# Hybrid decoder block on one core: the first modulation by quarters of its weight, half of each sum on the tensor engine, and x loaded first

## The chip, the cores and the metric

One program on one core of a Trainium2 chip. The metric is the device time of one execution in microseconds (us). PE is the tensor engine (PEld its weight loads), DVE the vector engine, ACT the scalar engine, POOL the GpSimd engine, SP the engine that issues almost all DMAs from one queue in program order.

## The reference

One decoder block on x of 1024 tokens by 1024 features, all float32. The change touches only its first lines:

```python
mod = (jax.nn.silu(c) @ w_ada[l] + b_ada[l]).astype(x.dtype)[:, None, :]
sh1, sc1, gt1, sh2, sc2, gt2 = jnp.split(mod, N_MOD, axis=-1)

h = rms_norm(x, g_pre_mix[l]) * (1.0 + sc1) + sh1
proj = h @ w_in[l]
```

c is one row of 1024 numbers, w_ada is 1024 x 6144. The columns 0 to 2047 of `mod` are sh1 (shift) and sc1 (scale): the first modulation, 8 MB of weight. `proj` then feeds sparse attention, a pooling mixer, a merge, the output projection and a squared-ReLU MLP of width 4096; those parts take all but about the first 80 us of 1478 and are not edited.

## The kernel before

The kernel is written for each engine as one program, with semaphores by name. Features lie in eight blocks of 128 (KT = 8, index k), tokens in two halves of 512 (CH).

What happens ahead of the projections, in order:

- SP loads c, sixteen pieces of w_ada (`ada_piece`: one k block by 1024 columns, 512 KB; scale part first), then four tiles of x (the first half of the tokens), the weight `wv_raw` of values and gates, the other four tiles of x, and two blocks of `w_in` into `raw`.
- DVE multiplies each piece by its 128 values of silu(c) and adds it to `ada_acc` [128 x 2048] (L1423). The sum over the 128 partitions is then made by PE in `mod_columns`: `ada_acc` as weights, a column of ones as the moving side (L2075), once for scale and once for shift, and DVE turns the result into `scale` and `shift`.
- ACT squares x with a running sum (`square_x`, L973), POOL makes the inverse root (`x_rstd_of`, L813 and L815), DVE multiplies x by it (`normalise_x`, L1415).
- PE transposes each block of four 128 x 128 squares (`x_transposes(n)`, n = 0 to 7 for the first half, 8 to 15 for the second, L2085). ACT applies scale and shift on the way out of PSUM (`h_tmp`, L998), DVE splits the result into `act_hi` and `act_lo` (`split_h`, L1439 and L1441), so that a float32 product can be made from three fp32r products.
- `values_and_gates(ch, k)`: 12 products of 280 columns (four token tiles by three, L2062 to L2064), for half 0 and all k, then half 1. `v_evict` and `v_split` empty the result.
- `project` makes the feature-major blocks a = 0, 1, ... for rotary, compression, pooling and gates. They need all of `act_hi` and `act_lo`, that is, everything above.

After the last transpose POOL clears `acc2` and SP starts the weight of the second modulation (L500), which DVE adds in between the projections.

The lines that set the order on PE are few:

```python
mod_columns(0)
for n in range(8):
    x_transposes(n)
pe.wait_ge(mod_done, 2)
for k in range(KT):
    pe.wait_ge(wv_lo_s, k // 2 + 1)
    values_and_gates(0, k)
```

A matmul call on two float32 operands that is no transpose (L2075, L2169) shows as two instructions in the trace; calls on fp32r operands and transposes show as one.

Of the kernel before, what the change touches and what calls it, by code (L numbers as in the profile page):

```python
# [21 lines left out]
P = 128  # L22
KT = D_MODEL // P
# [119 lines left out]
def hybrid_block(nc, A, out):  # L143
# [64 lines left out]
    ada = place("ada", 154, [P, 8, 1024], f32)  # L208
# [117 lines left out]
    ada_added, mod_mm, mod_done = sem("ada_added"), sem("mod_mm"), sem("mod_done")  # L326
# [113 lines left out]
    def _(sp):  # L440
# [14 lines left out]
        def ada_piece(n):  # L455
            if n >= 8:
                sp.wait_ge(ada_added, n - 7)
            k, part = n % KT, 1 - n // KT
            sp.dma_start(ada[:, n % 8, :], w_ada[k * P:(k + 1) * P, part * 1024:(part + 1) * 1024]) \
              .then_inc(wide_in[n % 8], 16)  # L460
# [20 lines left out]
        sp.wait_ge(ada_added, 16)  # L481
# [304 lines left out]
    def _(pool):  # L786
# [35 lines left out]
        for i in range(4):  # L822
# [3 lines left out]
            if i:  # L826
                x_rstd_of(3 + i)
        x_rstd_of(7)
# [123 lines left out]
    def _(act):  # L952
# [36 lines left out]

        act.wait_ge(wv_in, 32)  # L990
        wv_split(0)
        act.wait_ge(mod_done, 2)
        for n in range(2 * KT):
            act.wait_ge(xt_mm, n + 1)
            if n >= 2:
                act.wait_ge(h_lo, n - 1)
            k = n % KT
            act.activation(h_tmp[:, n % 2, :], ps[:, n % 4, :], ACT.Identity, scale=scale[:, k:k + 1],  # L998
                           bias=shift[:, k:k + 1]).then_inc(h_made, 1)
            if n < 3:  # L1000
                wv_split(n + 1)
            if 1 <= n < 5:
                square_x(n + 3)
# [395 lines left out]
    def _(dve):  # L1399
# [11 lines left out]
        dve.wait_ge(silu_steps, 3)  # L1411
        dve.wait_ge(acc_bias, 16)
# [4 lines left out]
        for n in range(16):  # L1417
            dve.wait_ge(wide_in[n % 8], 16 * (n // 8 + 1))
            if n % KT:
                dve.wait_ge(ada_added, n)  # L1420
            k, part = n % KT, 1 - n // KT
            sl = slice(part * 1024, (part + 1) * 1024)
            dve.scalar_tensor_tensor(out=ada_acc[:, sl], in0=ada[:, n % 8, :], scalar=silu_c[:, k:k + 1],  # L1423
                                     in1=ada_acc[:, sl], op0=ALU.mult, op1=ALU.add).then_inc(ada_added, 1)
            if n == 10:
                dve.wait_ge(mod_mm, 1)
                dve.wait_ge(g_pre_in, 16)
                dve.scalar_tensor_tensor(out=scale, in0=ps[:, 7, 8:16], scalar=1.0, in1=g_pre, op0=ALU.add,
                                         op1=ALU.mult).then_inc(mod_done, 1)
        for t in range(3):  # L1430
            normalise_x(t)
        dve.wait_ge(mod_mm, 2)
        dve.tensor_copy(shift, ps[:, 7, 0:8]).then_inc(mod_done, 1)
        normalise_x(3)
# [13 lines left out]
        for n in range(2 * KT):  # L1448
            split_h(h_tmp, n, h_made, h_hi, h_lo)
            if 4 <= n < 8:  # L1450
                normalise_x(n)
# [1032 lines left out]
```

## Time and profile before

| What | us |
|---|---|
| Median of 3 runs | 1479.71 (1479.65 to 1481.0) |
| The profiled execution, its own time | 1479.39 |
| Span of its trace | 1477.6 |
| PE busy in the trace | 1411.5 (96%) |
| DVE busy | 1072.4 (73%) |
| PE busy in the first 20 us | 0 |
| PE busy from 20 to 40 us | 10.79 |

The span is the profiled execution from its first to its last instruction, 1.8 us less than that execution's own time. Most of the span is PE working without a gap; the change lies in the first 80 us. The trace gives a granted clock of PE by stretch: 1.00 is 2.4 GHz, 0.50 is 1.2 GHz. It records no change of it before 44.5 us.

### The profile page before, as it was taken

How to read it: one execution, taken by the hardware profiler on the slowest of the kernel's cores; microseconds unless marked ns; L12 is line 12 of the kernel's file. 1: busy time of each engine (PE TensorE's matmuls, PEld its weight loads, DVE VectorE, ACT ScalarE, POOL GpSimd, SP SyncE). 2: the span in 40 equal slices, each digit the busy share in tenths (PEclk: the TensorE clock that was granted, in tenths of full speed). 3: DMA queues.
4: the chain of work that ended last, by engine and by line, in shares of the span. 5: the costliest groups of instructions: out<-in, count | busy, mean ns of one | idle time of the engine just before them, and what ended most of it. 6: DMA issues, size and time to landing. Idle time of an engine off the chain costs nothing.

```text
span 1477.6 us, 19523 instructions
## 1 busy us (share of the span) xinstructions
PE 1411.5 (96%) x7206; PEld 1181.3 (80%) x7206; DVE 1072.4 (73%) x1483; ACT 637.2 (43%) x1112; POOL 332.3 (22%) x429
## 2 busy tenths in 40 slices
PE   2897999999999999989999999999999999999997
PEld 2886878888888888768887877888888888888885
DVE  6668844677877878885432788877777797777778
ACT  1534434555665656663123664222222434343342
POOL 3324432333322322111210410000000030404034
PEclk9998999999999999999999999999999999999999
DMA  9377956322221211016453424544443773535226
GB/s 350 82 243 260 274 120 168 89 70 65 61 65 44 59 54 35 19 63 193 144 185 100 143 73 158 198 157 156 147 144 137 270 287 112 199 110 204 87 84 228
DMA packets 131750, 208.31 MB, mean 141 GB/s; under 512 B 19525, under 2 KB 84549, under 8 KB 128071
## 3 DMA queue, kind: packets, MB, share of 16 engines
q1 hardware_dynamic: 128074, 196.61, 40.3%
q0 software_dynamic: 3584, 10.49, 2.1%
q8 instruction: 56, 0.92, 0.3%
q14 instruction: 36, 0.29, 0.1%
HBM read 146.24 MB, written 54.53 MB: 136 GB/s over the span
## 4 chain that ended last, share of the span: by engine, by line
PE 84%; DVE 8%; issue 3%; ACT 2%; DMA 1%; SPq 1%; POOL 1%; DVEq 0%; POOLq 0%; ACTq 0%
PE ps L2062 19%; PE ps L2064 18%; PE ps L2063 18%; PE ps L2068 5%; PE ps L2070 5%; PE ps L2069 5%; PE ps L2257 4%; PE ps L2273 2%; PE ps L2274 2%; PE ps L2224 2%; PE ps L2225 2%; DVE pt_lo L1606 1%; DVE acc L1550 1%; DVE ada_acc L1423 1%; DVE negm L1615 1%
## 5 line engine op out<-in xcount | busy, mean ns | idle before, releaser
L2062 PE MATMUL ps<-act_hi,a_hi 128*128 128x512 f32 x448 | 190.9, 426 | 0.9 <-DVE a_lo L1402 0.9
L2064 PE MATMUL ps<-act_hi,a_lo 128*128 128x512 f32 x448 | 175.8, 392 | 0.0
L2063 PE MATMUL ps<-act_lo,a_hi 128*128 128x512 f32 x448 | 175.2, 391 | 0.0
L2062 PE MATMUL ps<-wr_hi,left_hi 128*128 128x512 f32 x320 | 124.5, 389 | 0.0
L2063 PE MATMUL ps<-wr_lo,left_hi 128*128 128x512 f32 x320 | 124.5, 389 | 0.0
L2064 PE MATMUL ps<-wr_hi,left_lo 128*128 128x512 f32 x320 | 124.5, 389 | 0.0
L1606 DVE TENSOR_TENSOR pt_lo<-ps,pt_hi 128x512 fp32r<-128x512 f32 (+1 forms) x160 | 102.9, 644 | 20.0 <-ACT pt_hi L1141 18.7
L1323 ACT ACTIVATE left_hi<-left_st 128x2048 fp32r<-128x2048 f32 x28 | 53.6, 1915 | 144.4 <-PE ps L2064 81.5
L1243 ACT ACTIVATE w_hi<-w1s 128x1024 fp32r<-128x1024 f32 x54 | 57.0, 1057 | 112.1 <-PE ps L2064 74.8
L1141 ACT ACTIVATE pt_hi<-ps 128x512 fp32r<-128x512 f32 (+1 forms) x160 | 89.0, 563 | 32.8 <-PE ps L2257 31.1
L1730 DVE TENSOR_TENSOR w_lo<-w1s,w_hi 128x1024 fp32r<-128x1024 f32 x54 | 65.9, 1221 | 51.1 <-ACT w_hi L1243 51.0
L1615 DVE TENSOR_REDUCE negm<-ps 128x1 f32<-128x640 f32 (+7 forms) x128 | 89.3, 698 | 18.1 <-PE ps L2230 17.9
L876 POOL TENSOR_SCALAR ssum<-ssum 128x1 f32<-128x1 f32 (+1 forms) x160 | 41.7, 261 | 265.8 <-ACT p_win L1122 137.0
L2064 PEld LDWEIGHTS ps<-act_hi,a_lo 128*128 128x128 f32 x448 | 84.2, 188 | 18.4
L929 POOL TENSOR_TENSOR y<-y,u 128x512 f32<-128x512 f32 x36 | 59.0, 1666 | 168.7 <-DVE u L1971 151.4
L2062 PEld LDWEIGHTS ps<-act_hi,a_hi 128*128 128x128 f32 x448 | 85.2, 190 | 12.8 <-issue 2.1
L2063 PEld LDWEIGHTS ps<-act_lo,a_hi 128*128 128x128 f32 x448 | 85.1, 190 | 9.4
L1899 DVE TENSOR_TENSOR left_lo<-left_st,left_hi 128x2048 fp32r<-128x2048 f32 x28 | 64.1, 2291 | 37.8 <-ACT left_hi L1323 37.8
L927 POOL COPY y<-u 128x512 f32<-128x512 f32 x12 | 13.1, 1123 | 345.5 <-DVE u L1971 342.7
L2062 PE MATMUL ps<-am_hi,w_hi 128*128 128x512 f32 x192 | 75.5, 393 | 1.0 <-ACT h2f L1208 1.0
L2064 PE MATMUL ps<-am_hi,w_lo 128*128 128x512 f32 x192 | 74.7, 389 | 0.0
L2063 PE MATMUL ps<-am_lo,w_hi 128*128 128x512 f32 x192 | 74.7, 389 | 0.0
(279 smaller groups left out, 3874.5 us busy)
## 6 DMA issues: line engine op xcount, KB each, us to landing
left_st<-h_dram SPq DMA_DIRECT2D x28, 1024.0 KB, 4.9
ada<-in_w_ada SPq DMA_DIRECT2D x48, 512.0 KB, 5.6
h_dram<-hid SPq DMA_DIRECT2D x48, 512.0 KB, 3.1
w1s<-in_w_fc SPq DMA_DIRECT2D x32, 512.0 KB, 4.4
w2s<-in_w_fc SPq DMA_DIRECT2D x16, 1024.0 KB, 7.6
raw<-in_w_in SPq DMA_DIRECT2D x28, 512.0 KB, 4.1
g_dram<-g_out POOLq DMA_DIRECT2D x32, 256.0 KB, 2.4
mg<-g_dram SPq DMA_DIRECT2D x16, 512.0 KB, 3.7
```

Of the source, the lines that this page charges most:

```text
L1141: act.activation(pt_hi[:, n % 3, 0:w], ps[:, 4 + n % 2, 0:w], ACT.Copy).then_inc(pthi, 1)
L1606: dve.tensor_tensor(pt_lo[:, n % 3, 0:w], ps[:, 4 + n % 2, 0:w], full(pt_hi[:, n % 3, 0:w]), ALU.subtract).then_inc(ptlo, 1)
L1615: dve.tensor_reduce(negm[:, n % 4, 0:1], src, AX.XY, ALU.min).then_inc(negm_done, 1)
L1730: dve.tensor_tensor(w1_lo[n % RING][:, :, :], src[:, :, :], full(w1_hi[n % RING][:, :, :]), ALU.subtract).then_inc(mlp_lo, 1)
L1899: dve.tensor_tensor(left_lo[n % STAGES][:, :, :], left_st[n % STAGES][:, :, :], full(left_hi[n % RING][:, :, :]), ALU.subtract).then_inc(m ...
L2062: pe.matmul(dst, wh, mh, start=start, stop=False)
L2063: pe.matmul(dst, wh, ml, start=False, stop=False)
L2064: return pe.matmul(dst, wl, mh, start=False, stop=stop)
L2068: pe.matmul(dst, wh, mh, start=False, stop=True, skip_group_check=True)
L2069: pe.matmul(dst, wh, ml, start=False, stop=True, skip_group_check=True)
L2070: return pe.matmul(dst, wl, mh, start=False, stop=True, skip_group_check=True)
L2257: ins = pe.transpose(at, src, ident[:, :])
```

## The change

The weight of the first modulation is cut into four quarters p (`ada_pair`): 256 columns of shift and 256 of scale, all eight k blocks, as four DMAs of 512 KB. Two quarters fit in the buffer; quarter p = 2 and 3 wait for the PE sums of quarter p - 2. x is loaded ahead of all of it.

Of each sum over k, the blocks 0 to 3 are multiplied on PE (the weight itself as the stationary side, silu(c) as one moving column), the blocks 4 to 7 on DVE as before, and PE adds the partition sums of DVE's part to the same PSUM columns (`mod_columns(p)`). A quarter gives scale and shift of two of the eight k blocks (`mod_pair(p)`).

The first half of x is transposed ahead of the modulation and stored as `x_t`; ACT then makes `h_tmp` from `x_t`, and also `act_hi` for that half. `values_and_gates(0, k)` runs as the k blocks come, with the four modulation quarters in between. The second half of x is squared after k = 3 on ACT, normalised on DVE ahead of the sums of quarter 2, and transposed from after k = 5 on.

```diff
+        def ada_pair(p):
+
+            if p >= 2:
+                sp.wait_ge(mod_mm, p - 1)
+            for half in range(2):
+                for part in range(2):
+                    at = part * 1024 + 256 * p
+                    sp.dma_start(ada[:, p % 2, part, 4 * half:4 * half + 4, :], w_ada[half * CH:half * CH + CH, at:at + 256]
+                                 .rearrange("(k p) n -> p k n", p=P)).then_inc(wide_in[4 * (p % 2) + 2 * half + part], 16)
...
-        for n in range(4):
-            ada_piece(n)
+        for t in range(4):
+            sp.dma_start(xt[:, t, :], x_v[:, t, :]).then_inc(x_arr[t], 16)
         sp.wait_ge(acc_zero, 1)
         sp.dma_start(ada_acc[0:1, :], b_ada[:, 0:2048]).then_inc(acc_bias, 16)
+        ada_pair(0)
...
-        for n in range(4, 16):
-            ada_piece(n)
-        for t in range(4):
-            sp.dma_start(xt[:, t, :], x_v[:, t, :]).then_inc(x_arr[t], 16)
         sp.dma_start(wv_raw[:, :, 0:P], w_in_v[:, :, C_VS:C_VS + P]).then_inc(wv_in, 16)
         sp.dma_start(wv_raw[:, :, P:WV_COLS], w_in_v[:, :, C_VW:C_VW + P + N_GATE]).then_inc(wv_in, 16)
+        ada_pair(1)
         for t in range(4, TT):
             sp.wait_ge(x_arr[t % 4], 16)
             sp.dma_start(xt[:, t, :], x_v[:, t, :]).then_inc(x_arr[t % 4], 16)
+        ada_pair(2)
+        ada_pair(3)
         for a in range(2):
             load_fm(a)
...
+        for n in range(KT):
+            act.wait_ge(xt_mm, n + 1)
+            act.activation(x_t[:, n, 0:CH], ps[:, n % 3, :], ACT.Copy).then_inc(xt_st, 1)
         act.wait_ge(wv_in, 32)
-        wv_split(0)
-        act.wait_ge(mod_done, 2)
+        for i in range(4):
+            wv_split(i)
         for n in range(2 * KT):
-            act.wait_ge(xt_mm, n + 1)
+            k = n % KT
+            if n >= KT:
+                act.wait_ge(xt_mm, n + 1)
+            elif k % 2 == 0:
+                act.wait_ge(mod_done, k + 2)
+                act.wait_ge(xt_st, k + 2)
             if n >= 2:
                 act.wait_ge(h_lo, n - 1)
-            k = n % KT
...
+            act.activation(h_tmp[:, n % 2, :], ps[:, n % 3, :] if n >= KT else x_t[:, k, 0:CH], ACT.Identity,
+                           scale=scale[:, k:k + 1], bias=shift[:, k:k + 1]).then_inc(h_made, 1)
+            if n < KT:
+                act.wait_ge(h_made, n + 1)
+                act.activation(act_hi[:, k, 0:CH], h_tmp[:, n % 2, :], ACT.Copy).then_inc(h_hi, 1)
+            if n == 3:
+                for t in range(4, TT):
+                    square_x(t)
...
+        def ada_sums(p):
+
+            for part in range(2):
+                dve.wait_ge(wide_in[4 * (p % 2) + 2 + part], 16 * (p // 2 + 1))
+            for k in range(4, KT):
+                n = 4 * p + k - 4
+                if n:
+                    dve.wait_ge(ada_added, n)
+                two = sums[:, :, 256 * p:256 * p + 256]
+                dve.scalar_tensor_tensor(out=two, in0=ada[:, p % 2, :, k, :], scalar=silu_c[:, k:k + 1], in1=two,
+                                         op0=ALU.mult, op1=ALU.add).then_inc(ada_added, 1)
+
+        def mod_pair(p):
+
+            dve.wait_ge(mod_mm, p + 1)
...
+        for t in range(4):
+            normalise_x(t)
+        dve.wait_ge(silu_steps, 3)
+        dve.wait_ge(acc_bias, 16)
+        for p in range(4):
+            if p in (1, 2):
+                for n in (2 * p - 2, 2 * p - 1):
+                    split_h(h_tmp, n, h_made, h_hi, h_lo)
+            if p == 2:
+                for t in range(4, TT):
+                    normalise_x(t)
+            ada_sums(p)
+            mod_pair(p)
+        for n in range(4, 2 * KT):
             split_h(h_tmp, n, h_made, h_hi, h_lo)
...
+        def mod_columns(p):
+
+            if p:
+                pe.wait_ge(mod_done, 2 * p)
+            else:
+                pe.wait_ge(xt_st, KT)
+            for part in range(2):
+                pe.wait_ge(wide_in[4 * (p % 2) + part], 16 * (p // 2 + 1))
+            for part in range(2):
+                for c in range(2):
+                    for k in range(4):
+                        pe.matmul(ps[:, 2 * part + c, 0:1], ada[:, p % 2, part, k, c * P:(c + 1) * P], silu_c[:, k:k + 1],
+                                  start=k == 0, stop=False)
+            pe.wait_ge(ada_added, 4 * p + 4)
+            for part in range(2):
+                for c in range(2):
+                    at = part * 1024 + 256 * p + c * P
+                    ins = pe.matmul(ps[:, 2 * part + c, 0:1], ada_acc[:, at:at + P], ones[:, 0:1], start=False, stop=True)
             ins.then_inc(mod_mm, 1)
...
+        for n in range(KT):
+            x_transposes(n)
+        pe.wait_ge(silu_steps, 3)
         mod_columns(0)
-        for n in range(8):
-            x_transposes(n)
-        pe.wait_ge(mod_done, 2)
         for k in range(KT):
             pe.wait_ge(wv_lo_s, k // 2 + 1)
             values_and_gates(0, k)
-            if k >= 4:
-                x_transposes(4 + k)
+            if k == 0:
+                mod_columns(1)
+            if k == 3:
+                mod_columns(2)
+                mod_columns(3)
+            if k == 5:
+                pe.wait_ge(mod_done, 8)
+                for n in range(KT, KT + 3):
+                    x_transposes(n)
         for k in range(KT):
-            if k < 4:
-                x_transposes(12 + k)
+            if k < 5:
+                x_transposes(KT + 3 + k)
             values_and_gates(1, k)
```

PE from its first instruction on, before (`ps<-ones,ada_acc` are the modulation's column sums, `ps<-ident,xt` transposes of x; a row here is a call, xN are N alike):

```order
L2075 MATMUL ps<-ones,ada_acc 128x1 [waits ada_added,consts_made]
L2075 MATMUL ps<-ones,ada_acc 128x1 x7
L2075 MATMUL ps<-ones,ada_acc 128x1 [waits mod_done,ada_added]
L2075 MATMUL ps<-ones,ada_acc 128x1 x7
L2085 MATMUL ps<-ident,xt 128x128 [waits x_norm]
L2085 MATMUL ps<-ident,xt 128x128 x15
```

PE after the 32 transposes of the first half, changed (`ps<-col,ada` are the products with the weight, 16 a quarter; the rows left out are the same three of `values_and_gates(0, 0)` for its other token tiles):

```order
L2110 MATMUL ps<-col,ada 128x1 [waits wide_in0,wide_in1,xt_st,silu_steps]
L2110 MATMUL ps<-col,ada 128x1 x15
L2116 MATMUL ps<-ones,ada_acc 128x1 [waits ada_added]
L2116 MATMUL ps<-ones,ada_acc 128x1 x3
L2089 MATMUL ps<-wv_hi,act_hi 128x280 [waits h_lo,wv_lo_s]
L2090 MATMUL ps<-wv_lo,act_hi 128x280
L2091 MATMUL ps<-wv_hi,act_lo 128x280
...
L2110 MATMUL ps<-col,ada 128x1 [waits wide_in5,wide_in4,mod_done]
L2110 MATMUL ps<-col,ada 128x1 x15
```

The transposes now stand ahead of the modulation, and 16 column calls in two groups have become 80 in four groups of 20, between and among the 280-column products.

DVE around the end of the modulation, before (`col<-ps` are scale and shift, `xt<-xt,col` is `normalise_x`):

```order
L1423 SCALAR_TENSOR_TENSOR ada_acc<-ada,col,ada_acc 128x1024 [waits ada_added,wide_in7]
L1415 TENSOR_SCALAR xt<-xt,col 128x1024 [waits x_rstd] x3
L1433 COPY col<-ps 128x8 [waits mod_mm]
L1415 TENSOR_SCALAR xt<-xt,col 128x1024 [waits x_rstd]
L1439 CAST act_hi<-h_tmp 128x512 [waits h_made]
L1441 TENSOR_TENSOR act_lo<-h_tmp,act_hi 128x512 [waits h_hi]
```

DVE from the splits of k = 2 and 3 to those of k = 4 to 7, changed:

```order
L1457 TENSOR_TENSOR act_lo<-h_tmp,act_hi 128x512 [waits h_hi,h_made] x2
L1425 TENSOR_SCALAR xt<-xt,col 128x1024 [waits x_rstd] x4
L1438 SCALAR_TENSOR_TENSOR ada_acc<-ada,col,ada_acc 128x2x256 [waits ada_added,wide_in3,wide_in2]
L1438 SCALAR_TENSOR_TENSOR ada_acc<-ada,col,ada_acc 128x2x256 [waits ada_added] x3
L1447 SCALAR_TENSOR_TENSOR col<-ps,col 128x2 [waits mod_mm]
L1449 COPY col<-ps 128x2
L1438 SCALAR_TENSOR_TENSOR ada_acc<-ada,col,ada_acc 128x2x256 [waits ada_added,wide_in7,wide_in6]
L1438 SCALAR_TENSOR_TENSOR ada_acc<-ada,col,ada_acc 128x2x256 [waits ada_added] x3
L1447 SCALAR_TENSOR_TENSOR col<-ps,col 128x2 [waits mod_mm]
L1449 COPY col<-ps 128x2
L1457 TENSOR_TENSOR act_lo<-h_tmp,act_hi 128x512 [waits h_hi,h_made] x4
```

The second half's four normalisations now stand between the splits of k = 2, 3 and the sums of quarter 2, and nothing of k = 4 to 7 is split until the sums and both column groups of quarters 2 and 3 are through.

## Rows read from the trace of the kernel before

**Rows 1.** The page, busy time of PE

```profile
PE 1411.5 (96%) x7206; PEld 1181.3 (80%) x7206; DVE 1072.4 (73%) x1483; ACT 637.2 (43%) x1112; POOL 332.3 (22%) x429
```

**Rows 2.** Chain of waits, 0 to 45 us: start, us, what

```profile
3.28 6.16 DMA ada_acc<-in_b_ada
...
20.94 6.39 DMA xt<-in_x
...
28.59 0.20 POOL col L813
...
34.94 0.56 POOL col L815
35.52 0.76 DVE xt L1415
```

**Rows 3.** Timeline of PE, 36 to 79 us: start, us, instruction, count, idle before

```profile
36.33 5.16 PE L2085 MATMUL ps<-ident,xt 128*128 128x128 f32 x24 [1.23 <-DVE xt L1415]
41.87 0.66 PE L2085 MATMUL ps<-ident,xt 128*128 128x128 f32 x4 [0.38 <-ACT h_tmp L998]
...
45.18 0.43 PE L2064 MATMUL ps<-wv_hi,act_lo 128*128 128x280 f32 x1
45.41 0.43 PE L2062 MATMUL ps<-wv_hi,act_hi 128*128 128x280 f32 x1
...
58.66 0.29 PE L2064 MATMUL ps<-wv_hi,act_lo 128*128 128x280 f32 x1
58.79 0.29 PE L2062 MATMUL ps<-wv_hi,act_hi 128*128 128x280 f32 x1
...
59.96 1.04 PE L2085 MATMUL ps<-ident,xt 128*128 128x128 f32 x8
...
78.64 0.39 PE L2062 MATMUL ps<-act_hi,a_hi 128*128 128x512 f32 x1
```

**Rows 4.** Groups by line and shape, 0 to 110 us: busy us, mean ns, idle before

```profile
L998 ACT ACTIVATE h_tmp<-ps,col 128x512 f32<-128x512 f32 x16 | 12.5, 780 | 13.9 <-PE ps L2085 10.5 <-DVE act_lo L1441 3.4
...
L1441 DVE TENSOR_TENSOR act_lo<-h_tmp,act_hi 128x512 fp32r<-128x512 f32 x16 | 11.1, 692 | 0.6
...
L973 ACT ACTIVATE junk<-xt 128x1024 f32<-128x1024 f32 x8 | 8.4, 1056 | 24.5 <-DMA xt<-in_x 24.2
...
L2075 PE MATMUL ps<-ones,ada_acc 128*128 128x1 f32 x32 | 7.1, 352 | 28.0 <-DVE ada_acc L1423 28.0
...
L1415 DVE TENSOR_SCALAR xt<-xt,col 128x1024 f32<-128x1024 f32 x8 | 6.0, 749 | 1.4 <-POOL col L815 1.4
...
L1031 ACT ACTIVATE vc_f<-ps 128x512 f32<-128x512 f32 x2 | 1.2, 598 | 6.8 <-PE ps L2064 6.8
```

**Rows 5.** Instructions of one line, L1015 (ACT, SBUF to fp32r): ns min/median/max

```profile
L1015 ACT ACTIVATE r_hi<-r_cos x12: 615/630/638, 122.2 to 213.0; 128x512 fp32r<-128x512 f32 x12
```

**Rows 6.** DMAs issued by L459, from issue to landing

```profile
DMA to landing us min/median/max: 4.4/6.0/8.8
```

**Rows 7.** Timeline of PE, the second modulation's column sums

```profile
186.71 3.73 PE L2169 MATMUL ps<-ones,acc 128*128 128x1 f32 x32
```

**Rows 8.** Windows of PE: stretch, its us, PE busy and count, granted clock, DMA share, GB/s

```profile
44.00:45.00 1.00, 0.87 (x6) 0.77 0.84 6
...
47.00:48.00 1.00, 1.00 (x7) 0.52 0.33 68
48.00:49.00 1.00, 1.00 (x9) 1.00 0.88 211
...
191.00:192.00 1.00, 1.00 (x3) 0.66 0.00 0
```

**Rows 9.** Groups by shape on DVE: the nearest to a sum over 2 x 256

```profile
L1713 DVE SCALAR_TENSOR_TENSOR m_a<-mg,ps 128x512 f32<-128x512 f32 x16 | 11.0, 686 | 22.8 <-PE ps L2064 20.8 <-issue 2.1
```

**Rows 10.** Timelines of SP and DVE after the last transpose

```profile
75.02 1.75 SPq L500 DMA_DIRECT2D ada<-in_w_ada  x4
...
86.72 0.69 DVE L1471 TENSOR_TENSOR r_cos<-ps,cos 128x512 f32<-128x512 f32 x1 [2.02 <-ACT r_swap L1027]
```

More of the change, by code:

```diff
@@ L207, in hybrid_block @@
     h_tmp = place("h_tmp", 146, [P, 2, CH], f32)
-    ada = place("ada", 154, [P, 8, 1024], f32)
+    ada = place("ada", 154, [P, 2, 2, KT, 256], f32)
+    x_t = place("x_t", 64, [P, KT, SEQ], f32)
     acc2 = place("acc2", 96, [P, 4, 1024], f32)
@@ L325, in hybrid_block @@
     wv_in, wv_hi_s, wv_lo_s = sem("wv_in"), sem("wv_hi_s"), sem("wv_lo_s")
[L326 removed]
+    ada_added, xt_st, mod_mm, mod_done = sem("ada_added"), sem("xt_st"), sem("mod_mm"), sem("mod_done")
     x_arr = [sem(f"x_arr{i}") for i in range(4)]
@@ L478, in _ @@
             sp.dma_start(xt[:, t, :], x_v[:, t, :]).then_inc(x_arr[t % 4], 16)
+        ada_pair(2)
+        ada_pair(3)
         for a in range(2):
             load_fm(a)
-        sp.wait_ge(ada_added, 16)
+        sp.wait_ge(mod_mm, 4)
         with nc.allow_non_contiguous_dma(reason="a few columns"):
@@ L825, in _ @@
                                full(wv_hi[:, 2 * i:2 * i + 2, :]), ALU.subtract).then_inc(wv_lo_s, 1)
-            if i:
-                x_rstd_of(3 + i)
-        x_rstd_of(7)
+        for t in range(4, TT):
+            x_rstd_of(t)
         pool.wait_ge(xt_mm, 2 * KT)
@@ L1415, in normalise_x @@
             dve.tensor_scalar(xt[:, t, :], xt[:, t, :], msq[:, t:t + 1], None, ALU.mult).then_inc(x_norm, 1)
[L1417 to L1426, printed above, removed]
-                dve.wait_ge(g_pre_in, 16)
[L1428 to L1434, printed above, removed]
+        sums = ada_acc[:, :].rearrange("p (f n) -> p f n", f=2)
+        def ada_sums(p):
[10 more added lines that the diff above has]
+            dve.wait_ge(mod_mm, p + 1)
+            if p == 0:
+                dve.wait_ge(g_pre_in, 16)
+            two = slice(2 * p, 2 * p + 2)
+            dve.scalar_tensor_tensor(out=scale[:, two], in0=ps[:, 2:4, 0], scalar=1.0, in1=g_pre[:, two],
+                                     op0=ALU.add, op1=ALU.mult).then_inc(mod_done, 1)
+            dve.tensor_copy(shift[:, two], ps[:, 0:2, 0]).then_inc(mod_done, 1)
         def split_h(src, n, made, hi_s, lo_s):
@@ L1438, in split_h @@
             dve.wait_ge(made, n + 1)
-            dve.tensor_copy(act_hi[:, k, sl], src[:, n % 2, :]).then_inc(hi_s, 1)
+            if n >= KT:
+                dve.tensor_copy(act_hi[:, k, sl], src[:, n % 2, :]).then_inc(hi_s, 1)
             dve.wait_ge(hi_s, n + 1)
@@ L1446, in v_split @@
                               full(v_st[:, t, :, 0:64]), ALU.subtract).then_inc(v_lo, 1)
-        for n in range(2 * KT):
+        for t in range(4):
[7 more added lines that the diff above has]
+            if p == 2:
+                for t in range(4, TT):
+                    normalise_x(t)
+            ada_sums(p)
+            mod_pair(p)
+        for n in range(4, 2 * KT):
             split_h(h_tmp, n, h_made, h_hi, h_lo)
-            if 4 <= n < 8:
-                normalise_x(n)
             if 8 <= n < 12:
@@ L2070, in three_more @@
             return pe.matmul(dst, wl, mh, start=False, stop=True, skip_group_check=True)
-        def mod_columns(part):
-            for n in range(8 * part, 8 * part + 8):
-                ins = pe.matmul(ps[:, 7, n:n + 1], ada_acc[:, n * P:(n + 1) * P], ones[:, 0:1], start=True, stop=True)
+        def mod_columns(p):
[15 more added lines that the diff above has]
+                    ins = pe.matmul(ps[:, 2 * part + c, 0:1], ada_acc[:, at:at + P], ones[:, 0:1], start=False, stop=True)
             ins.then_inc(mod_mm, 1)
@@ L2081, in x_transposes @@
                 pe.wait_ge(x_norm, 4 * ch + 4)
-            if n >= 4:
-                pe.wait_ge(h_made, n - 3)
+            if n >= 3:
+                pe.wait_ge(xt_st if n < KT + 3 else h_made, n - 2)
             for t in range(4):
-                ins = pe.transpose(ps[:, n % 4, t * P:(t + 1) * P], xt[:, 4 * ch + t, k * P:(k + 1) * P], ident[:, :])
+                ins = pe.transpose(ps[:, n % 3, t * P:(t + 1) * P], xt[:, 4 * ch + t, k * P:(k + 1) * P], ident[:, :])
             ins.then_inc(xt_mm, 1)
@@ L2101, in _ @@
         pe.wait_ge(consts_made, CONSTS)
-        pe.wait_ge(ada_added, 8)
-        mod_columns(1)
-        pe.wait_ge(ada_added, 16)
-        pe.wait_ge(mod_done, 1)
+        for n in range(KT):
+            x_transposes(n)
+        pe.wait_ge(silu_steps, 3)
         mod_columns(0)
-        for n in range(8):
-            x_transposes(n)
-        pe.wait_ge(mod_done, 2)
         for k in range(KT):
@@ L2202, in _ @@
                 mix(a - 9)
-        pe.wait_ge(mod_done, 4)
+        pe.wait_ge(mod_done, 10)
         gate_part(0, range(KT))
```

14 lines of the change are left out of this document (removed).

## The prediction

> **What bounds the kernel now.** I began with the page's busy times: PE is busy 96% of the span [rows 1], so time can only be won where PE still waits, and any PE work put on the chain is paid in full. The chain of waits of the first 45 us says where it waits [rows 2]. Read it as relay legs: the bias and the first weight pieces land at 9.4 us, DVE then adds sixteen pieces while SP queues behind it, the first tile of x lands only at 27.3 (20.94 + 6.39), POOL makes four inverse roots from 28.6 to 35.5, DVE normalises the last tile until 36.3, and PE begins its transposes. The timeline of PE [rows 3] gives the marks that I use below: transposes from 36.33, value products from 44.6, the end of the first half (of `values_and_gates(0, 7)`) at 59.96, and the first projection, a product of 512 columns, at 78.64. From 59.96 to 78.64 is 18.7 us. From 78.64 on nothing in the program is edited, and I follow the change up to that mark.
>
> **Two speeds of PE.** The same timeline has one 280-column product every 0.23 us at 45 us and every 0.13 us at 58 us; the windows [rows 8] show why: a granted clock of 0.5 (1.2 GHz) until just before 48, then 1.00 (2.4 GHz). The 24 transposes from 36.33 take 0.215 us each, so half clock too, though the window still prints 1.00 there; from 41.87 four take 0.66 together, full clock. The column sums that the change multiplies have a price at either level: 32 instructions (16 calls) in 7.1 us, 0.222 each, in the first modulation [rows 4], and 32 in 3.73 us, 0.117 each, in the second, which comes straight after dense products [rows 7]. Soon after that stretch, at 191 us, the clock falls [rows 8]. So these short instructions are dear and do not keep the clock up. A call is two instructions: the new `mod_columns(p)` with 20 calls is 40, which is 4.7 us at full clock and 8.9 at half. Before there were 32 in all; now there are 160, from 18.7 to 35.5 us in place of 7.1.
>
> **The new start, leg by leg.** The four x tiles take the queue place of the first four weight pieces; the bias behind those landed at 9.4 [rows 2], and the first piece 4.4 us after its issue at 1.3 [rows 6], so tile 0 lands at 5.7. A square and its read take 1.25 us (1.06 for the square [rows 4]), so POOL starts at 7.0. In the old trace its four roots took 6.9 us (28.6 to 35.5): 13.9, and 0.75 for the last normalisation gives 14.7. 32 transposes at 0.215 take 6.9: 21.6; moving the last block out costs 0.35 until ACT starts and 0.6 for a copy of that shape [rows 4]: PE may start quarter 0 at 22.6. Its weight is there by about 15 (4.2 MB ahead of it or in it, at 0.5 MB per 1.3 us behind the mark of 9.4), and DVE's four sums by 18: the sum over 2 x 256 is not in the old trace; the nearest row has 0.69 for 512 elements [rows 9], 0.72 with its gap, 2.9 for four.
>
> Quarter 0: between 4.7 and 8.9; it starts near full clock after the transposes and loses it, so I take 7.2: 29.8. Then DVE makes two columns each of scale and shift (0.35), ACT makes `h_tmp` (0.78 [rows 4]) and `act_hi` (0.63 for that form [rows 5]), DVE `act_lo` (0.69 [rows 4]), 2.6 with the handovers: products of k = 0 start at 32.4, twelve at 0.23: 35.2. That is 12 us sooner than now, and all the change wins.
>
> Quarter 1 is queued on PE right behind k = 0. Its clock depends on whether 2.8 us of products brought it back: bounds 4.7 and 8.9, I take 6.5, the middle: 41.7. PE goes on with k = 1 to 3, 36 products between 4.6 and 8.4; the old trace needed 3.4 us of such products from 44.5 to get the full clock, so about 3 us slow and the rest fast, 6.1: 47.8.
>
> Now DVE is late, not PE. After quarter 1 (41.7) come 0.35 for the columns and two blocks of 0.78 + 0.63 on ACT: 45.1. Only then does ACT square the four tiles of the second half, 4 x 1.27: 50.2. The last root costs 1.5 to 2 more on POOL, 52.0; DVE normalises, 52.8. The sums of quarter 2 stand behind that normalisation in DVE's order: 2.9, 55.7. PE has made the 16 product calls of quarter 2 meanwhile (at most 7.1 from 47.8, 54.9), and after an idle stretch pays its last 8 instructions at half clock, 1.8: 57.5, and 0.35 for the columns: 57.9. Quarter 3 uses the same PSUM columns, so PE could not begin it earlier: all 40 instructions on the path, at half clock, 8.9: 66.8. `split_h(4)` is queued on DVE behind `mod_pair(3)`, though its scale was known at 57.9: 0.35 + 0.7 more, and k = 4 starts at 67.9. 24 products (3.1 us slow, then 11 fast, 4.5), 12 transposes at full clock (1.5) and 24 products (3.1) make 9.1: the first half ends at 77.0, not at 59.96.
>
> From there the second half has the same work as before, five blocks of transposes and 96 products: 18.7 with its own slow stretch. First projection at 95.7, 17.1 us later than 78.64.
>
> What else moves costs nothing. The second modulation's loads wait for the last transpose, which now comes one k later, some 1.6 us; DVE's first projection work has 2.0 us of idle ahead of it at 86.72 [rows 10], which covers it; without that cover it is 1.6. The constants' loads start at 66.8 and must be through by about 92; weight quarter 3 is issued at 41.7 and needed at 57.9. ACT's `act_hi` in place of DVE's lies inside the 2.6 above.
>
> The sum: the profiled execution took 1479.39, and 17.1 more is 1496.5; the median of the three runs is 0.3 higher, 1496.8, rounded to **1497**.
>
> **A page against the trace.** Rows 3 show transposes at half clock from 36.33 and at full clock by 41.87, with nothing but transposes between. The Trainium skill, "TensorE: Matmul & The Clock Gate", Part 4 (PE-mode transpose), says that transposes do not count as busy for the gate. By it quarter 0 would run wholly at half clock, and the sum would be 1.7 us more, 1498.5. The trace disagrees, so I keep 7.2; either lies inside the forecast's own range.
>
> **The rivals.**
> The clock stays up. For it: 280-column products lie between the quarters. Against it: the fall at 191 [rows 8] after 32 such sums. All at full clock, the marks become 27.3 for quarter 0, 31.5 for k = 0, 36.1 for quarter 1, 39.4 for ACT, 50.0 for the sums of quarter 2 (the same 10.6 behind), 51.3, 56.0 for quarter 3, 64.8 for the first half: 4.8 late, 1484.5. Chance 0.13.
>
> The clock never comes back inside the modulation: quarters 0 and 1 at 8.9 and k = 1 to 3 slow. Only what lies ahead of ACT's squares counts: 1.7 + 2.4 more, 1501. Chance 0.12, as the old trace brought the clock back within 5 us of dense work.
>
> The other side: the new products are cheaper than their rows, because weight loads for a run of calls into one PSUM column overlap. The price is that of `mod_columns`, four times on the path. At 0.055 us an instruction, half of the full-clock price, a quarter is 2.2; the marks are 24.8, 30.2, 32.4, 46.3, 47.2, 49.4, and 59.6 for the first half: even. Below 0.055 it is faster; at 0.03 about 4 us, 1476. Against it: old and new calls have the same shapes, and both old groups take much the same number of cycles an instruction, 266 at half clock and 281 at full. Chance 0.07.
>
> That the change does not start PE early, because the first x tiles land no sooner than now, would cost 12 us more, 1509; the landing of the first pieces at 4.4 us after their issue [rows 6] leaves it 0.01.
>
> **How the numbers follow.** Forecast as summed, 1490 to 1500: 0.59. Clock never back, 1500 to 1504: 0.12. Clock up, 1483 to 1486: 0.13. A mix of the two clocks below my middle, 1486 to 1490: 0.08. Cheap products, 1473 to 1482: 0.07, of which 0.04 faster by more than the measurement can tell. No early start: 0.01. The range is 1485 to 1503: it takes in the forecast, the mix, most of the slow-clock case and an edge of the fast one. A measurement here can tell about 0.2%, 3.0 us, from no change: faster by more 0.04, within 0.03, slower 0.93.
>
> **What would show it.** Right: transposes from about 15 us, k = 0 at 32, four column groups of 5 to 9 us, a granted clock of 0.5 in most of 30 to 75, one long gap of the 280-column products between k = 3 and k = 4, some 48 to 68 us, and the first projection at 96. Wrong: a first projection before 80, column instructions well under 0.117 us, or PE through with quarter 3 by 56.

## The result and the profile after

The changed kernel takes 1497.57 us (median of 4 runs, 1493.26 to 1498.04) against 1480.36 for the kernel before in the same rounds: ratio 1.0108, 95% interval 1.0087 to 1.0129, slower by 17 us. Timed again with other kernels it gave 1497.69 against 1481.05, 1.0118 [1.0102, 1.0133]. The prediction was 1497.0.

The profiled execution took 1497.61, its span is 1495.8, 18.2 longer than before, and PE is busy 1439.5 us with 7334 instructions, 28 us and 128 instructions more than [rows 1]. The 128 are 160 column instructions in place of 32. The timeline of PE answers to [rows 3] (start, us, instruction, count, and the idle time ahead with what ended it):

```profile
12.74 6.41 PE L2126 MATMUL ps<-ident,xt 128*128 128x128 f32 x32 [12.74 <-DVE xt L1425]
19.93 5.31 PE L2110 MATMUL ps<-col,ada 128*128 128x1 f32 x32 [0.78 <-issue]
25.11 1.84 PE L2116 MATMUL ps<-ones,ada_acc 128*128 128x1 f32 x8
29.66 0.57 PE L2089 MATMUL ps<-wv_hi,act_hi 128*128 128x280 f32 x1 [2.71 <-DVE act_lo L1457]
...
32.60 6.82 PE L2110 MATMUL ps<-col,ada 128*128 128x1 f32 x32
39.28 1.84 PE L2116 MATMUL ps<-ones,ada_acc 128*128 128x1 f32 x8
...
47.83 3.63 PE L2110 MATMUL ps<-col,ada 128*128 128x1 f32 x32
54.50 1.86 PE L2116 MATMUL ps<-ones,ada_acc 128*128 128x1 f32 x8 [3.05 <-DVE ada_acc L1438]
56.68 6.99 PE L2110 MATMUL ps<-col,ada 128*128 128x1 f32 x32 [0.32 <-DVE col L1449]
63.53 1.85 PE L2116 MATMUL ps<-ones,ada_acc 128*128 128x1 f32 x8
66.39 0.57 PE L2089 MATMUL ps<-wv_hi,act_hi 128*128 128x280 f32 x1 [1.01 <-DVE act_lo L1457]
...
75.34 0.60 PE L2126 MATMUL ps<-ident,xt 128*128 128x128 f32 x4
...
94.75 0.39 PE L2089 MATMUL ps<-act_hi,a_hi 128*128 128x512 f32 x1
```

The x32 rows with 128x1 are the products of a quarter, the x8 rows its closing columns. k = 0 starts 15 us earlier than in [rows 3] (29.66 against 44.6), and from there to the first projection PE needs 65.1 us where it needed 34.1. The windows (stretch, its us, PE busy and count, granted clock, DMA share, GB/s) show half clock from 22 to 44 us and from 54 to 68 us:

```profile
20.00:22.00 2.00, 2.00 (x18) 0.94 1.10 351
22.00:44.00 22.00, 19.29 (x89) 0.50 0.76 259
46.00:52.00 6.00, 5.45 (x48) 1.00 1.06 306
54.00:68.00 14.00, 12.17 (x55) 0.50 0.07 4
```

The same 32 products took 6.82 and 6.99 us at 0.50 (quarters 1 and 3) and 3.63 at 1.00 (quarter 2). The timeline of DVE shows what quarter 2's closing columns wait for from 51.45 on: the second half's tiles, released one by one by POOL, and only then the four sums.

```profile
46.26 0.76 DVE L1425 TENSOR_SCALAR xt<-xt,col 128x1024 f32<-128x1024 f32 x1 [1.19 <-POOL col L819]
...
50.67 0.75 DVE L1425 TENSOR_SCALAR xt<-xt,col 128x1024 f32<-128x1024 f32 x1 [0.71 <-POOL col L819]
51.33 3.11 DVE L1438 SCALAR_TENSOR_TENSOR ada_acc<-ada,col,ada_acc 128x512 f32<-128x512 f32 x4
```

### The profile page after: what moved, and what is told of

Its sections match the earlier page's. It is cut to its first block, busy times and chain, and to the rows that moved or that the text cites. A ratio compares the mean times of both kernels' runs of the same rounds, so it can differ in the third digit from the quotient of the medians.

```text
span 1495.8 us, 19792 instructions
## 1 busy us (share of the span) xinstructions
PE 1439.5 (96%) x7334; PEld 1208.8 (81%) x7334; DVE 1059.6 (71%) x1481; ACT 646.9 (43%) x1128; POOL 327.2 (22%) x429
## 4 chain that ended last, share of the span: by engine, by line
PE 84%; DVE 8%; ACT 3%; issue 2%; SPq 1%; DMA 1%; POOL 0%; DVEq 0%; POOLq 0%; ACTq 0%
PE ps L2089 18%; PE ps L2091 18%; PE ps L2090 18%; PE ps L2095 5%; PE ps L2097 4%; PE ps L2096 4%; PE ps L2301 4%; PE ps L2317 2%; PE ps L2318 2%; PE ps L2268 2%; PE ps L2269 2%; PE ps L2110 1%; DVE pt_lo L1633 1%; DVE acc L1577 1%; DVE negm L1642 1%
## 5 line engine op out<-in xcount | busy, mean ns | idle before, releaser
L1633 DVE TENSOR_TENSOR pt_lo<-ps,pt_hi 128x512 fp32r<-128x512 f32 (+1 forms) x160 | 103.0, 644 | 20.0 <-ACT pt_hi L1153 18.7
L2089 PEld LDWEIGHTS ps<-act_hi,a_hi 128*128 128x128 f32 x448 | 85.6, 191 | 14.7 <-DVE a_lo L1414 3.1
```

The lines of the kernel that those rows point to most:

```text
L1633: dve.tensor_tensor(pt_lo[:, n % 3, 0:w], ps[:, 4 + n % 2, 0:w], full(pt_hi[:, n % 3, 0:w]), ALU.subtract).then_inc(ptlo, 1)
L2089: pe.matmul(dst, wh, mh, start=start, stop=False)
```

## The experiments

All ratios are to the kernel before in the same rounds, whose median was 1480.36 in the first and between 1479.81 and 1481.12 in the others. Two marks of PE's timeline describe each trace: the start of the first value product (k = 0) and of the first projection.

| Kernel | k = 0 | first projection | median us | ratio, 95% |
|---|---|---|---|---|
| before | 44.56 | 78.64 | 1480.36 | |
| changed | 29.66 | 94.75 | 1497.57 | 1.0108 [1.0087, 1.0129] |
| changed, second trace | 26.66 | 89.03 | 1497.69 | 1.0118 [1.0102, 1.0133] |
| no products | 25.45 | 82.76 | 1485.2 | 1.0026 [1.0016, 1.0036] |
| squares early | 29.76 | 91.26 | 1491.56 | 1.0065 [1.004, 1.009] |
| all sums on DVE | 25.46 | 91.84 | 1494.44 | 1.009 [1.007, 1.0109] |
| filler | 29.38 | 97.02 | 1504.21 | 1.0165 [1.0128, 1.0201] |
| order alone | 41.15 | 80.91 | 1483.32 | 1.0016 [1.0006, 1.0026] |
| order alone, transposes late | 40.84 | 80.11 | 1483.65 | 1.0022 [1.0013, 1.0031] |
| two shift groups | 40.33 | 76.42 | 1480.0 | 0.9991 [0.9981, 1.0001] |
| two rows by products | 38.57 | 76.20 | 1478.42 | 0.9979 [0.997, 0.9989] |
| the same, transposes late | 38.45 | 74.80 | 1477.89 | 0.9983 [0.9974, 0.9992] |
| the same, normalise ahead | 38.47 | 72.46 | 1475.13 | 0.9965 [0.9953, 0.9977] |
| before, the two moves | 44.70 | 78.23 | 1479.64 | 1.0001 [0.9992, 1.001] |

**1. No products.** In `mod_columns(p)`:

```diff
-                    for k in range(4):
-                        pe.matmul(ps[:, 2 * part + c, 0:1], ada[:, p % 2, part, k, c * P:(c + 1) * P], silu_c[:, k:k + 1],
-                                  start=k == 0, stop=False)
```

> The changed kernel without the sixteen product calls of each quarter: the rows of k = 0 to 3 are left out of the first modulation's sum, all else (loads, the vector engine's four sums for k = 4 to 7, the four closing columns, transposes first) stays. My theory, that the products and closers which PE issues on its own path are what the change costs: quarter 0 is 1.8 us and not 7.0, and with it every wait behind it moves up; k = 0 starts at about 24 instead of 29.7 us, quarter 1 falls from 8.4 to about 2, and quarters 2 and 3 then wait for the vector engine (four sums, 3.1 us each, behind the second half's squares), so k = 4 starts near 50.5 instead of 66.4 and the first projection near 79 instead of 94.75. Whole kernel: 1481 to 1482 us, 16 us below the changed kernel and level with the kernel before. Rival A, the late thing is the weight's last quarters from DRAM (their four loads are issued behind the x tiles): then the products only fill a wait, k = 4 stays near 66 and the time stays at 1495 to 1498. Rival B, the vector engine's sums and the round trip between quarters are the path and the products lie beside them: quarters 2 and 3 each keep a wait of about 3 us and the gain is only quarter 0 and 1, 5 to 11 us: 1486 to 1492.

Measured: 12 us less than the changed kernel (1.0108 less 1.0026), not 16. The work of the products is most of the loss (this kernel leaves half of each sum out, and run 3 shows what that half costs elsewhere); Rival A falls, Rival B is partly right. PE's timeline of this kernel shows the waits that the products had covered:

```profile
30.25 1.84 PE L2114 MATMUL ps<-ones,ada_acc 128*128 128x1 f32 x8 [1.66 <-DVE ada_acc L1438]
...
45.56 1.84 PE L2114 MATMUL ps<-ones,ada_acc 128*128 128x1 f32 x8 [6.08 <-DVE ada_acc L1438]
50.83 1.84 PE L2114 MATMUL ps<-ones,ada_acc 128*128 128x1 f32 x8 [3.43 <-DVE ada_acc L1438]
```

k = 4 starts at 53.67, 3.2 later than I had written, and that was lost by k = 1: the sums of quarter 1 stand behind DVE's two splits, which took 3.27 us together at 23.81 where [rows 4] has 0.69 each. POOL's four subtractions for `wv_lo` (5.80 us from 20.74), which stand back to back in the changed kernel, ran beside them.

**2. Squares early.** In ACT's and DVE's programs:

```diff
-            if n == 3:
+            if n == 1:
                 for t in range(4, TT):
                     square_x(t)
...
+            ada_sums(p)
-            if p == 2:
+            if p == 1:
                 for t in range(4, TT):
                     normalise_x(t)
-            ada_sums(p)
```

> The changed kernel with one thing moved: ACT squares the second half of x after the h of k = 1 instead of k = 3, and DVE normalises the second half's tiles ahead of the second quarter's modulation copies instead of behind the two splits. Theory: PE's 3.05 us wait for ada_acc before quarter 2's closing columns (54.50 us) is the second half's squares, roots and normalisation, which DVE has in front of its sums of quarter 2; moved up by about 8 us they leave the path, the closers follow the products at 51.5, the first projection comes 3 us earlier and the kernel takes about 1494.3. Rival: the second half's tiles have not landed by then, or quarter 1's copies now wait behind the normalisation and k = 1 to 3 are late by what is saved: 1497 to 1500.

Measured: in the trace the closing columns stand at 51.47 with no wait and the first projection comes 3.5 us earlier, as expected. The whole is 6 us faster than the changed kernel by the ratios (0.0043 of 1480), which the two intervals make uncertain by 5. The wait of 3.05 was real and needed only another order.

**3. All sums on DVE.** The product calls are gone as in run 1, and DVE sums all eight row blocks:

```diff
-            for k in range(4, KT):
+            for k in range(KT):
...
-            pe.wait_ge(ada_added, 4 * p + 4)
+            pe.wait_ge(ada_added, 8 * p + 8)
```

> The changed kernel with all eight row blocks of each quarter summed by the vector engine and PE left with the four closing columns of each quarter; the numbers computed are the same. Theory: the vector engine then has eight sums of 0.77 us (6.2 us) per quarter where PE had about 7 us of products, and it starts on the next quarter without waiting for PE: quarter 0 ends at about 25, but quarters 2 and 3 come one behind the other from the vector engine (6.2 + 0.7 us each plus normalisation), so k = 4 starts near 64.3 instead of 66.4 and the time is about 1495.5. If the products on PE were hidden, as the rival of the first run has it, this is slower than the changed kernel by the added sums, 4 x 3.1 us on the path: 1503 or more.

Measured: k = 4 at 63.41 (expected 64.3), 1494.44 (expected 1495.5). The rival (1503) falls. PE now waits 10.09 and 6.68 us for DVE ahead of the closing columns of quarters 2 and 3:

```profile
52.05 1.83 PE L2115 MATMUL ps<-ones,ada_acc 128*128 128x1 f32 x8 [10.09 <-DVE ada_acc L1439]
...
60.56 1.83 PE L2115 MATMUL ps<-ones,ada_acc 128*128 128x1 f32 x8 [6.68 <-DVE ada_acc L1439]
```

The kernel is still no slower than the changed one (3 us less, uncertain by 4), so in the changed kernel the products do not relieve DVE: they take its place on the path. Of the 12 us of run 1, then, some 9 are the price of having this half of the sums on the path at all, whichever engine makes it: run 3, which makes all of them on DVE, is 9 us slower than run 1.

**4. Filler.** A wide bf16 product of constants behind each narrow call (76 of them; the expectation says 80):

```diff
+            pe.matmul(ps[:, 0, 1:CH], ident_b[:, :], mask_cmp[:, :, :].rearrange("p t n -> p (t n)")[:, 1:CH], start=False, stop=True,
+                      skip_group_check=True)
```

> The changed kernel with one 511-column bf16 product of constants put behind every product and closer call of the quarters, 80 in all, into columns of the same banks that nothing reads; the result is unchanged. What it tests: in the quarters the granted clock is 0.50 and an instruction of the one-column calls takes 0.222 us, while at full clock it is 0.117 us. If the clock follows what PE streams, wide products between the narrow ones keep it at 1.00: a pair of column instructions then takes 0.23 us and the filler 0.22 us, so a call takes about what it took (0.45 us), the transposes and first products of the second half run at full clock as well, and the time is 1493 to 1498. If the clock does not follow it, the filler costs 0.43 us on top of each call that is on the path, about 80 x 0.43 = 34 us less what quarters 2 and 3 spend waiting: 1517 to 1530. A result between says that only part of the stretch is at full clock.

Measured: both rules were half right. The windows of this kernel:

```profile
20.00:40.00 20.00, 16.92 (x140) 1.00 0.88 300
...
52.00:66.00 14.00, 13.68 (x63) 0.50 0.00 0
```

Through quarters 0 and 1 the clock stayed at 1.00, and quarter 1 with its filler took 6.9 us (30.99 to 37.84) against 8.4 without. Then PE waited 1.7 us for DVE from 49.67, the clock fell, and 14 us of the same mixed stream, PE busy 13.68 of them, ran at 0.50: there a call with its filler took 0.67 us and a call alone takes 0.43, so the filler cost 0.24 us a call; at full clock it was 0.35 with and 0.22 alone. The result is 7 us slower than the changed kernel by the medians and 8 by the ratios, uncertain by 6, as its four times lie apart (1499 to 1510 us). In this one trace the mixed stream went with a full clock for 20 us, but it did not bring the clock back once it had fallen.

**5. The changed kernel again.**

> The changed kernel unchanged, timed once more in the same rounds as the runs below, so that the differences to it are taken on one chip. First measurement: ratio to before 1.0108 with interval 1.0087 to 1.0129. Expected 1.009 to 1.0125 again, 1495 to 1499 us, with the first projection near 94.8 us in the trace; if its clock falls and rises at other places than in the first trace, the marks behind k = 1 move by up to 4 us and show how much of the loss is the clock's phase.

Measured: the same median, but the profiled execution took 1492.96. It is the cleanest price of the clock in this study, the same program with two clocks. They part already in the 32 transposes, which took 5.49 us here and 6.41 in the first trace. PE's timeline of this second trace:

```profile
19.05 3.70 PE L2110 MATMUL ps<-col,ada 128*128 128x1 f32 x32 [0.86 <-issue]
22.61 1.34 PE L2116 MATMUL ps<-ones,ada_acc 128*128 128x1 f32 x8
...
29.60 3.82 PE L2110 MATMUL ps<-col,ada 128*128 128x1 f32 x32
...
48.38 1.87 PE L2116 MATMUL ps<-ones,ada_acc 128*128 128x1 f32 x8 [2.73 <-DVE ada_acc L1438]
50.57 6.99 PE L2110 MATMUL ps<-col,ada 128*128 128x1 f32 x32 [0.32 <-DVE col L1449]
```

Products of quarters 0 and 1 took 7.52 us here and 12.13 in the first trace; the first projection is 5.7 us earlier and the execution 4.65 shorter. One of four times was like this in both measurements of the kernel (1493.26 and 1492.96 us).

**6. The order alone**, from the kernel before: x first, transposes first into `x_t`, then the sixteen 1024-column sums on DVE. In PE's program (KPE is 0 here and 2 in run 9; the arguments of `mod_columns` are a PSUM bank and the first and last column):

```diff
-        mod_columns(0)
         for n in range(8):
             x_transposes(n)
+        pe.wait_ge(xt_st, KT)
+        pe.wait_ge(ada_added, 8)
+        mod_columns(0, 8, 16)
+        pe.wait_ge(ada_added, 16 - KPE)
+        pe.wait_ge(mod_done, 1)
+        mod_columns(2, 0, 8)
```

> The kernel before with one half of the change: x is loaded first, its first four tiles are normalised and transposed first and stored as x_t, and the weight follows in the sixteen 128 x 1024 pieces of before, all summed on the vector engine; the shift columns come after the last sum as before. No quarters and no product by weight blocks. Theory (the order is worth a little, the quarters and their products are what costs): the vector engine's sums end at about 34.8 us, the eight shift columns take 3.55 at half clock, h and its split follow, and k = 0 starts at about 41 instead of 44.6 us: about 3.6 us off, 1476 to 1477.5. Rival: the weight, which now lands behind 2 MB of x, is what the sums wait for, and the last sum ends at 37 or later: k = 0 at 43 to 45 and the time level with before, 1479 to 1481; then the order alone brings nothing, and all 16 us of the change's loss are the quarters'.

Measured: k = 0 at 41.15 as expected, and yet 2 us slower than before. The next rows are of the kernel before (DVE), then of this one (DVE and PE):

```profile
35.14 0.17 DVE L1433 COPY col<-ps 128x8 f32<-128x8 f32 x1 [0.33 <-PE ps L2075]
...
53.15 0.75 DVE L1415 TENSOR_SCALAR xt<-xt,col 128x1024 f32<-128x1024 f32 x1
```

```profile
38.80 0.17 DVE L1462 COPY col<-ps 128x8 f32<-128x8 f32 x1 [3.67 <-PE ps L2103]
...
54.77 0.75 DVE L1440 TENSOR_SCALAR xt<-xt,col 128x1024 f32<-128x1024 f32 x1
```

```profile
55.62 1.09 PE L2113 MATMUL ps<-ident,xt 128*128 128x128 f32 x4 [4.01 <-issue]
```

The shift comes 3.7 us later, since DVE's sums start at 13.20, behind the four normalisations, and not when the bias and the first pieces land at 9.4 [rows 2]. Everything that starts with it (h, splits, the second half's normalisation) is late too, so PE stops for 4.01 us before the second half's transposes and resumes at half clock. From k = 0 to the first projection it takes 39.8 us in place of 34.1: an earlier k = 0 is not an earlier end.

**7. The same with the transposes behind k = 5.**

```diff
-            if k == 4:
+            if k == 5:
                 pe.wait_ge(mod_done, 2)
-            if k >= 4:
-                x_transposes(4 + k)
+                for n in range(KT, KT + 4):
+                    x_transposes(n)
```

> The order alone (x first, transposes first, all sums on the vector engine) with one thing moved: PE transposes the second half's first four blocks after the values of k = 5 and not after k = 4 and between the following ones. Theory: in the run of the order alone k = 0 did start 3.5 us earlier, and PE then gave it back in a wait of 4.01 us before the second half's first transposes, because the vector engine's splits and normalisation start only when the shift arrives (38.80 instead of 35.14 us). With k = 5 in front of that wait, 1.6 to 2.8 us of it are filled: 1480.5 to 1481.7, against 1483.3. Rival: the splits of k = 5 to 7 come as late as the transposes and the wait only changes its name: 1483 to 1484.

Measured: 1.0022, no better than the 1.0016 of run 6. The wait shrank to 2.21 and the clock fell elsewhere (mean 0.66 in 62 to 72 us), behind three waits of 0.8 us for `v_st`. The expected gain did not come.

**8. Two shift groups.**

```diff
-        mod_columns(2, 0, 8)
+        mod_columns(2, 0, 2)
+        mod_columns(3, 2, 8)
```

> As the run above, but the shift's columns are closed in two groups, columns 0 and 1 first (in a PSUM bank of their own), then 2 to 7, so that h of k = 0 and 1 starts behind two columns (0.9 us) and not eight (3.55 us). Theory: k = 0 starts 2.6 us earlier than in that run and the other six columns, which PE issues while ACT and DVE make h of k = 0, are hidden: 1473.5 to 1475. Rival: PE's later work sets the pace (k = 2 and on wait for h, 1.1 to 1.4 us each), and the 2.6 us are given back: no more than 1 us better than that run.

Measured: 3.3 us less than run 6, against an expected 2.6, and level with the kernel before. The range of 1473.5 to 1475 was missed by 5 us, mostly since it was built on the time that run 6 was expected to take. k = 0 itself moved only 0.8, because DVE's copy of the six other columns stands ahead of its first split; the last normalisation moved 2.3 (52.48). PE waits 2.89 us ahead of the second half's transposes and, unlike in run 6, goes on at full clock:

```profile
53.33 0.63 PE L2115 MATMUL ps<-ident,xt 128*128 128x128 f32 x4 [2.89 <-issue]
```

**9. Two rows by products.**

```diff
+        for n in range(KT):
+            for k in range(KPE):
+                ins = pe.matmul(ps[:, 1, n:n + 1], ada[:, ROT + k, n * P:(n + 1) * P], silu_c[:, k:k + 1],
+                                start=k == 0, stop=k == KPE - 1)
```

> As the run above, and of the shift's sum the rows of k = 0 and 1 are taken off the vector engine: PE adds them up by sixteen one-column product calls between the transposes and the scale's columns, where it waits for the vector engine anyway; the other 14 pieces stay sums. Theory: products cost nothing where PE waits and only the vector engine's two sums (2 x 1.22 us or so) come off the path: k = 0 starts at about 36 us, 1471 to 1473. Rival: the scale's columns now come behind the products and a weight piece that lands late, or the pieces' rotation with six places holds the loads back, and the time is that of the run above or up to 3 us more.

Measured: 0.9979, clearly below the kernel before and 1.6 us less than run 8, which the intervals leave uncertain by 2; the expected 1471 to 1473 did not come, and k = 0 stands at 38.57, not 36.

```profile
19.59 5.84 PE L2143 MATMUL ps<-col,ada 128*128 128x1 f32 x32 [0.79 <-ACT x_t L1009]
25.29 3.55 PE L2108 MATMUL ps<-ones,ada_acc 128*128 128x1 f32 x16
32.21 3.57 PE L2108 MATMUL ps<-ones,ada_acc 128*128 128x1 f32 x16 [3.37 <-DVE ada_acc L1454]
```

The sixteen product calls cost nothing, as they lie where PE waits for DVE (the scale's columns behind them start 1.0 us later than in run 8, and DVE does not wait for them), and the last sum ends at 32.1 and not 35.1. The rest was held back by DVE's order again, and by a first split of 1.74 us in place of 0.69. This is the change's own idea, made where PE is idle, and there it does no harm and probably helps.

**10 and 11. Transposes late, then normalise ahead of the split.**

```diff
         for n in range(2 * KT):
+            if 4 <= n < 8:
+                normalise_x(n)
             split_h(h_tmp, n, h_made, h_hi, h_lo)
-            if 4 <= n < 8:
-                normalise_x(n)
```

> The run with two shift rows by products and the shift closed in two groups, with the second half's first four transposes moved behind k = 5 in the same way. Theory: its wait of 2.24 us before those transposes is filled by k = 5 at full clock (1.6 us instead of 2.8), k = 8 starts near 57 instead of 60.1 and the time is 1475.5 to 1476.5 against 1478.4, 0.3% below before. Rival: ACT and the vector engine set the second half's pace (h, split and value eviction of each block), and what is gained at k = 8 is waited for at k = 9 to 12: 1478.

> As the run above, and the vector engine normalises each of the second half's tiles ahead of the split beside it instead of behind it. Theory: the last tile is ready at about 50 and not 51.5 us, so the transposes follow k = 5 with no wait: 0.5 to 0.8 us less than that run, 1475 to 1476. Rival: each split is 0.8 us later, k = 5 itself starts later, and the two cancel: level with that run.

Measured: 1477.89, no clear gain, and 1475.13, 0.35% below the kernel before. In the last one the transposes start at 50.52 with no wait:

```profile
50.52 1.91 PE L2118 MATMUL ps<-ident,xt 128*128 128x128 f32 x16
```

From k = 0 to the first projection it takes 34.0 us, as in the kernel before; with waits of 1.26 (run 10) and 2.24 (run 9) it took 36.4 and 37.6, and each of these two has a stretch at half clock after the wait. The length of the wait alone does not settle it: run 8 waited 2.89 us, kept the full clock and needed 36.1, and run 7 waited 2.21 and needed 39.3.

**12. The two moves in the kernel before.**

> The kernel before, with nothing of the change, and only the two small moves of the last two runs: PE transposes the second half's first four blocks after k = 5, and the vector engine normalises each second-half tile ahead of the split beside it. It tells how much of the last run's 0.35% below before belongs to the early transposes, the two shift groups and the two rows by products, and how much to the two moves alone. In the trace of before PE waits 1.2 us for the last normalised tile at 53.95 us. Theory: the moves are worth that wait and no more here, 1479.5 to 1480.3, level with before or 0.1% below it, and the other 4 to 5 us are the early shift's. Rival: the moves are the whole gain: 1475 to 1476.

Measured: 1.0001. The rival falls: the moves alone are worth nothing here (uncertain by 1.3 us). Of the 5 us of run 11, run 9 has 3 without the moves, and the other 2 need the earlier shift and the moves together. My reason was misread: the wait of 1.2 us is at 36.33 [rows 3], and before the transposes of 53.95 PE never waited.

## Why the prediction was right

The time was within 1 us of the median, and the cause was the one given: column instructions on PE's own path, mostly at half clock. By the ratios, the order alone is +2 us and the rest of the change adds 14 to 15, of which run 1 gives 12 to the work of the products. What the prediction did not say, and run 3 shows, is that the same sums on DVE would cost nearly as much. That rest of the change is more than the quarters (ACT also makes `act_hi`, and the second half of x is squared later), and only the late squares were tried by themselves (run 2). That the sum came so near is in part luck: terms wrong by 2 us each, in both directions, cancelled.

- **The new start.** Summed to 14.7, measured 12.74. The four roots took 5.2 us and not 6.9. POOL did nothing else between them in either kernel. In [rows 2] the second operation of a root (`L815`) takes 1.63 us beside DVE's sums, 0.94 beside a normalisation and 0.55 where DVE stands still; here, where DVE has no sums yet, it takes 0.55 each time. The transposes took 6.41 for 6.9.
- **Quarter 0**, 7.2 predicted, 7.0 measured, beginning at full clock (0.94 in 20 to 22 us). k = 0 came at 29.66, not 32.4, all from the start.
- **Quarter 1** was the mis-sized term: 6.5 was taken as the middle (the middle of 4.7 and 8.9 is 6.8), and 8.4 measured, near the upper bound. The second trace has 5.3. The clock after k = 0 is one or the other, so a middle is the value that neither trace shows. The early start (2.6 us) was eaten by this (1.9) and by k = 1 to 3 (6.8 for 6.1), and k = 3 ended at 47.8, as written.
- **DVE late at quarter 2**: closing columns at 54.5, predicted 55.7; run 2 took this wait away and gained its length in the trace.
- **Quarter 3** 8.7 for 8.9; k = 4 at 66.4 for 67.9; the first half ends at 75.3 for 77.0.
- **The second half** took 19.4 and not 18.7, with three waits of 0.8 us for `v_st`, of which the kernel before has the same three, the first only 0.32 long: first projection at 94.75 for 95.7.
- **"What else moves costs nothing"** does not fit this trace, which is 2.1 us longer behind the first projection; that made up for the 1 us above. The chain of waits has, after and then before:

```profile
118.57 5.57 SPq L542
...
129.29 7.40 DMA ada<-in_w_ada
```

```profile
102.30 5.03 SPq L538
...
112.33 6.45 DMA ada<-in_w_ada
```

The issue and the landing of the second modulation's weight took 1.5 us longer, and the sums on DVE behind them are what PE waits for at 159.11. From the first projection to the end is 1399.0 us before and 1400.7 to 1402.3 in the six traces of kernels by quarters (the changed one twice, runs 1 to 4). But it is also 1400.7 in run 12 and 1401.1 in run 7, which have no quarters, and 1399.3 in run 11, so that the 2 us come from the change is not shown; why those transfers are slower was not tried.
- **The rivals.** "The clock stays up" lives in part: the second trace has it in the products of quarters 0 and 1, with half clock between them, and one time in four is as short, 4.7 us less and never 12. "Clock never back" fits the first trace from 22 to 45 us and fails there. "Cheap products" is out: 3.63 us for 32 is 0.113 an instruction at full clock and 6.99 is 0.218 at half, as in [rows 4] and [rows 7]. By the rule of the Trainium skill, "TensorE: Matmul & The Clock Gate", Part 4 (PE-mode transpose), quarter 0 would have begun at half clock behind 32 transposes; the trace disagrees, with a granted clock of 0.94 in 20 to 22 us and 1.00 in the second trace. As the windows print 1.00 also over the slow transposes before, the durations are the better sign: quarter 0's 32 products took 3.70 us in the second trace, 0.116 each, which is the full-clock price.

## What to carry to other kernels

Work moved onto the busiest engine is free only where that engine waits anyway: product calls of the same shape cost up to 12 us in the quarters (64 of them, on the path) and nothing in run 9 (16, in a wait). When the first step of a stage is brought forward, follow the last thing that the stage needs (here the shift, and DVE's order behind it) before counting a gain. Where PE's clock may be at either level, forecast two cases and not their middle, and ask which short wait decides between them.

## What the runs showed of the hardware

- One program ran with two clocks in the same place: quarter 1's 32 products took 6.82 us in one execution and 3.82 in another. PE's instructions ahead of them were the same, and stood up to 3 us earlier in the second, where also the 32 transposes (5.49 against 6.41 us) and quarter 0's products (3.70 against 5.31) were faster.
- In the filler's trace a dense stream stayed at half clock from 52 to 66 us, while in the changed kernel the 280-column products that begin at 41.0 had it back by 46 (1.00 in 46 to 52 us). What tells the two apart is open.
- A one-column pair behind a 511-column product started its successor 0.13 us later at full clock; pairs one behind another take 0.23. That the wide product covers the pair's weight load is argued, not shown.
- DVE's split took 1.6 us a piece instead of 0.69 while POOL's subtractions on other tiles were running (run 1, at 23.81 us). The other way round, POOL's one-column `L815` took 1.63 us instead of 0.55 beside DVE's sums in the kernel before.
